# Natural feature order for the gathered tokens: a strided stationary operand in place of strided copies

## What is computed

```python
h = h + rms_norm(mix, post_mix_norm[l])
ffn = hier_moe(rms_norm(h, pre_ffn_norm[l]), ...)      # 32 experts, 2 of them per token, and a shared expert
h = h + rms_norm(ffn, post_ffn_norm[l])
...
a = jnp.einsum('nd,edf->nef', t, w_gate)
b = jnp.einsum('nd,edf->nef', t, w_up)
hid = jax.nn.silu(a) * b * combine[:, :, None]
routed = jnp.einsum('nef,efd->nd', hid, w_down)
```

## Time and profile before

| | |
|---|---|
| median of 3 runs | 901.75 us (901.68 to 901.86) |
| span of the profiled execution, first to last instruction | 899.0 us |
| TensorE matmul busy | 808.3 us (90%), mean granted clock 0.965 |
| TensorE weight loads busy | 641.8 us (71%) |
| VectorE busy | 487.2 us (54%) |
| ScalarE busy | 381.4 us (42%) |
| GpSimd busy | 48.4 us (5%) |
| chain that ended last | TensorE 70%, DMA 16%, VectorE 6%, ScalarE 4% |

### The profile page before, as it was taken

One profiled execution on the slowest core, in us unless ns is written; L12 is line 12 of the kernel. 1 busy time (PEld: TensorE's weight loads), 2 busy tenths in 40 slices (PEclk: granted clock), 3 DMA queues, 4 the chain that ended last, 5 costly groups with the idle time before them and its releaser, 6 DMA issues.

```text
span 899.0 us, 13430 instructions
## 1 busy us (share of the span) xinstructions
PE 808.3 (90%) x5498; PEld 641.8 (71%) x5498; DVE 487.2 (54%) x805; ACT 381.4 (42%) x643; POOL 48.4 (5%) x114
## 2 busy tenths in 40 slices
PE   6989999997777576779999998999999999999995
PEld 5968778764444233449989885558887999999974
DVE  6786658411110030065936585776667666666675
ACT  5564558210000100055456845655444544444454
POOL 5000030101010001000000000000000000000000
PEclk9998999999898889899999999999999999999998
DMA  9951163799999999997418554127555555555101
GB/s 282 375 194 47 48 262 136 298 405 421 423 420 421 421 421 421 414 348 217 144 43 333 181 194 152 48 96 256 160 169 177 186 188 189 187 188 194 51 1 47
DMA packets 76974, 205.81 MB, mean 229 GB/s; under 512 B 5720, under 2 KB 48896, under 8 KB 64624
## 3 DMA queue, kind: packets, MB, share of 16 engines
q1 hardware_dynamic: 68430, 150.44, 47.1%
q0 software_dynamic: 8480, 54.49, 14.9%
q10 hardware_dynamic: 2, 0.00, 0.0%
HBM read 203.87 MB, written 1.05 MB: 228 GB/s over the span
## 4 chain that ended last, share of the span: by engine, by line
PE 70%; DMA 16%; DVE 6%; ACT 4%; issue 2%; SPq 0%; POOL 0%; ACTq 0%; DVEq 0%
DMA big<-in_w_up 13%; PE ps L2044 10%; PE ps L2045 9%; PE ps L2046 9%; PE ps L1838 9%; PE ps L1840 8%; PE ps L1839 8%; PE ps L2157 4%; DMA big<-in_w_down 3%; PE ps L2138 1%; PE ps L2171 1%; DVE WL L1130 1%; PE ps L2393 1%; ACT WH L645 1%; PE ps L2330 1%
## 5 line engine op out<-in xcount | busy, mean ns | idle before, releaser
L1130 DVE TENSOR_TENSOR WL<-big,WH 128x1024 fp32r<-128x1024 f32 x154 | 186.6, 1223 | 105.9 <-ACT WH L645 105.0
L645 ACT ACTIVATE WH<-big 128x1024 fp32r<-128x1024 f32 x154 | 160.5, 1054 | 70.5 <-PE ps L2046 70.0
L1838 PE MATMUL ps<-XH,WH 128*128 128x256 f32 (+1 forms) x640 | 187.4, 293 | 1.6 <-DVE WL L1122 0.7
L1840 PE MATMUL ps<-XH,WL 128*128 128x256 f32 (+1 forms) x640 | 183.2, 286 | 0.0
L1839 PE MATMUL ps<-XL,WH 128*128 128x256 f32 (+1 forms) x640 | 183.1, 286 | 0.0
L1838 PEld LDWEIGHTS ps<-XH,WH 128*128 128x128 f32 x640 | 123.6, 193 | 7.1 <-issue 3.9
L1839 PEld LDWEIGHTS ps<-XL,WH 128*128 128x128 f32 x640 | 123.7, 193 | 0.8
L1840 PEld LDWEIGHTS ps<-XH,WL 128*128 128x128 f32 x640 | 123.6, 193 | 0.0
L2157 PE MATMUL ps<-big 128*32 128x256 f32 x1024 | 74.6, 456 | 45.1 <-DMA big<-in_w_gate 28.5
L2044 PE MATMUL ps<-WH,XH 128*128 128x512 f32 x240 | 97.7, 407 | 2.1 <-ACT big L983 1.3
L2157 PEld LDWEIGHTS ps<-big 128*32 128x32 f32 x1024 | 42.2, 130 | 78.7 <-issue 67.7
(11 more groups left out here) (395 smaller groups left out, 1090.3 us busy)
## 6 DMA issues: line engine op xcount, KB each, us to landing
big<-in_w_in SPq DMA_DIRECT2D x35, 1024.0 KB, 9.5
big<-in_w_gate SPq DMA_DIRECT2D x16, 1024.0 KB, 14.9
big<-in_w_up SPq DMA_DIRECT2D x16, 1024.0 KB, 15.6
big<-in_w_gate POOLq DMA_DIRECT2D x16, 1024.0 KB, 18.6
big<-in_w_up POOLq DMA_DIRECT2D x16, 1024.0 KB, 20.1
big<-in_w_down SPq DMA_DIRECT2D x16, 1024.0 KB, 16.2
big<-in_w_down POOLq DMA_DIRECT2D x16, 1024.0 KB, 20.2
big<-in_w_mlp_up SPq DMA_DIRECT2D x16, 1024.0 KB, 5.5
```

The lines of the kernel that those rows point to most:

```text
L645: s.activation(dst, src, ACT.Copy).then_inc(ev("unit_high"), 1)
L1130: v.tensor_tensor(dst, src, h.bitcast(F32), ALU.subtract).then_inc(ev("unit_split"), 1)
L1838: mm(o, h, rh, start=first, stop=False, skip_group_check=skip)
L1840: return mm(o, l, rh, start=False, stop=last, skip_group_check=skip)
```

## The change

The copy at line 841 is now contiguous on both sides: `h_tok` holds the features in their natural order. The residual at line 1604 (1603 after the change) reads and writes contiguous rows. The gather takes chunk c out of `h_tok` by a view `eighth`, columns c, c + 8, c + 16 and so on: 128 words with a step of 8 words (32 bytes). The values of all results are the same. No instruction is added, removed or moved on any engine.

```diff
-        by_row = lambda a: a.rearrange("p (c q) -> p q c", c=DC)
-        in_order = lambda a: a.rearrange("p (q c) -> p q c", c=DC)
+        eighth = lambda a, c: a.rearrange("p (q c) -> p c q", c=DC)[:, c, :]
...
-                s.activation(by_row(h_tok[:, t, :]), in_order(h1[:, t, :]), ACT.Copy, scale=st(5, t))\
+                s.activation(h_tok[:, t, :], h1[:, t, :], ACT.Copy, scale=st(5, t))\
                     .then_inc(ev("t_by_row"), 1)
...
-                v.scalar_tensor_tensor(out=in_order(ffn_tmp[:, t, :]), in0=by_row(h_tok[:, t, :]), scalar=st(4, t),
-                                       in1=in_order(ffn_tmp[:, t, :]), op0=ALU.mult, op1=ALU.add)\
+                v.scalar_tensor_tensor(out=ffn_tmp[:, t, :], in0=h_tok[:, t, :], scalar=st(4, t),
+                                       in1=ffn_tmp[:, t, :], op0=ALU.mult, op1=ALU.add)\
                     .then_inc(ev("h_ffn"), 1)
...
-                        last = mm(o, h_tok[:, t, c * P:(c + 1) * P], sel[:, b, t, first:first + width].bitcast(F32),
+                        last = mm(o, eighth(h_tok[:, t, :], c), sel[:, b, t, first:first + width].bitcast(F32),
                                   start=t == 0, stop=t == TT - 1)
```

## The result

The changed kernel takes 912.03 us (median of 5 runs, 910.44 to 914.24) against 901.75 us: the ratio is 1.0108 with a 95% interval of 1.0089 to 1.0127. The forecast was 908.4 us, in a range up to 911.0. The direction was right; the loss is larger than the upper end of the range by 1 us.

What follows compares the result with a forecast made beforehand. TensorE was taken to bound up to about 198 us, then DMA; 6.8 us (first gathers) + 0.2 (256-column gathers) - 0.3 (tail) = +6.7 us, forecasting 908.4 us, range 900.3 to 911.0.

Steps and rivals of the forecast that it cites:

- The stage: Up to about 198 us TensorE binds and its delay reaches the loads whole; afterwards DMA bounds and covers slower gathers.
- The size of a strided load: Gather loads with a step of 8 words: doubled, 107 ns more each, 6.8 us over the two first gathers' 64 loads.
- The upper end, 1.93 ns per word: Gather loads: ScalarE's strided-write extra on top of 0.84 ns per word, 247 ns instead of 107, total 911.0 us.
- Rival A: Gather loads cost nothing more with a step; only the tail's 0.3 us remains, 901.4 us; chance 0.24.
- The gathers with 256 columns: Two groups ahead of 198 us: loads hide behind matmuls save the first of each group, 0.2 us more.
- The tail: After the experts: a cheaper residual at line 1604 brings line 1838 0.3 us earlier; bounds 0 and nearer 1.46 us.
- TensorE's return: TensorE restarting at 395.00 us in the tail, taken as set by TensorE itself and not by line 1604.
- The range: Whole kernel: 8 in 10 range of 900.3 to 911.0 us, taking in A and B and leaving out C.
- B: Gather loads cost line 2164's extra of 58 ns each: +3.4 us, 905.2 us; chance 0.14.
- C: Gather loads cost three times the 107 ns: +15.0 us, 916.8 us; chance 0.12.

Runs made afterwards that it cites:

- third experiment: Changed kernel with the 8-word step only in the 80 gather loads from 198 us on, earlier gathers reading contiguously: 901.56 us, ratio 0.9988.
- the second: Changed kernel with the gather's operand read contiguously again, keeping only the contiguous copy and residual: 902.13 us, ratio 0.9991.

## Why the prediction was wrong

- *The stage.* That TensorE binds up to the third quad's gates, that its delay reaches DMA whole there, and that later gathers are covered: right. The stage grew by 8.67 us for 8.66 us of gathers, and the 80 later loads cost nothing (third experiment).
- *The size of a strided load.* This is the term that was mis-sized. I took a doubling, 107 ns per load and 6.8 us; measured were 8.07 / 64 = 126 ns of pace and 8.07 us. (The load's own duration grew by 334 - 190 = 144 ns, where 107 was forecast; the pace of the gather grew by less.) The upper end, 1.93 ns per word and 140 ns per load, was nearer. The argument for the doubling was wrong too: I drew the doubling from line 2164, whose loads with a step of 2 words are 58 ns dearer than those of line 2226, and held that the trace disagrees with the rule of lines of 16 bytes. But those loads turn tiles; the gather's ordinary loads at the same step take 196 ns, 6 more than contiguous ones. For them the rule of the Trainium skill (SBUF — State Buffer, Specifications (TRN2)) holds in its threshold: two hits on a line are enough (196 ns at a step of 2 words), one is not (329 ns at 4). The other rule of the Trainium skill, a load as its columns divided by 1.2 GHz (TensorE: Matmul & The Clock Gate, LDWEIGHTS), has no term for a step: the trace agrees with its slope for contiguous columns (0.84 ns) and is 6 ns over the contiguous load at a step of 2, but some 60 to 180 ns over it from 3 words on. Rival A, that an ordinary load notices no step, so holds at 2 words and falls at the 8 of this change.
- *The gathers with 256 columns.* 0.2 us forecast for the two groups, 0.59 measured (0.29 + 0.30): the eight loads and matmuls of a group take 2.23 and 2.29 us where they took 1.94 and 1.99, so the longer load is not quite hidden.
- *The tail.* 0.3 us forecast, 0.2 measured. TensorE's return was rightly taken as not set by line 1604.
- *The range.* 6.8 + 0.2 - 0.3 became 8.07 + 0.59 - 0.2 = 8.5 us, 910.2 us, still inside. So the mis-sized terms make 1.8 of the 3.6 us by which the median lies over the forecast. What left the range is the other 1.8 us of the median, for which the forecast had no term: it took every stage but the changed ones as unchanged in each execution. With fillers in the wait behind the first gather the changed kernel stands at 911.0 and 910.58 us, at the range's end and inside it; the cause of this part stays open.
- *The rivals.* B's 58 ns per load came from the wrong kind of load. C's threefold load did not come; its neighbours at other steps go up to 372 ns.

## What to carry over

A strided operand is not free because it removes strided copies: ask on which engine the copies lie, and what hides them. Here 1.9 us on ScalarE were hidden and of 1.46 us on VectorE 0.2 arrived, while the step went to the engine that bound the stage. A load with a step of 2 words kept its speed within 6 ns; no kernel with such a layout was run. And ask how wide the matmul behind a load is: the same slow load cost 0.126 us with 128 columns, 0.03 us with 256 and nothing under DMA.

## What was not expected of the hardware

- Turning loads and ordinary loads pay for a step differently: with 2 words 198 against 140 ns for the former, 196 against 190 ns for the latter. With the step both kinds take about the same time.
- A step of 12 words (372 ns) is dearer than 16 (305 ns) and 8 (337 ns); from 4 words on the cost does not follow the step's size.
- The granted clock can fall to 0.5 in a wait of 1.44 us after a strided gather of 7.61 us. Without fillers this stands in one profile of three; after contiguous gathers of 3.58 us and the same wait it stands in none of three (the kernel before, the second and the third experiment).
